# All large SBUF buffers moved by 128 bytes, and the two halves of a rounded weight pair set 4352 bytes apart

## The chip, the cores and the metric

One Trainium2 chip, one of its cores. The time is the device time of one execution in microseconds (us), from runs on the chip. Before the change: median 2161.43 us of 3 runs, 2159.44 to 2162.81.

## What is computed

Two layers of one kind of block, then one layer of another kind, on 512 tokens of width 1024, all in float32.

```python
for l in range(DEPTH):                       # DEPTH = 2
    proj = rms_norm(x, norm1[l]) @ w_in[l]   # 1024 -> 3148 columns, cut into the inputs of four attentions
    ...                                      # latent, sliding-window, top-k-selected and forget-gated attention
    x = x + mixed @ w_out[l]                 # 1024 x 1024
    x = x + jnp.square(jax.nn.relu(rms_norm(x, norm2[l]) @ w_up[l])) @ w_down[l]   # 1024 x 4096, 4096 x 1024
x = rms_norm(x, final_norm)
# second block, one layer
proj = (rms_norm_2(x, norm_w) * (1.0 + scale) + shift) @ w_in_2    # 1024 -> 9232 columns
y_a = gated_delta_rule(...) @ w_proj_a       # 8 heads, chunks of 64 tokens
y_b = dilated_window_attention(...) @ w_proj_b
x = x + gate * ((sigmoid(ga) * y_a + sigmoid(gb) * y_b) @ w_out)
```

The products with weight matrices are most of the work. The rest (norms, softmax, the delta rule's small matrices) is untouched by the change, apart from where its buffers lie.

## The kernel before

**A product in three.** A float32 operand is kept as two fp32r numbers, `high` (the value rounded) and `low` (what rounding left over). `product` (lines 179 to 183) makes a product out of three matmuls that add up in PSUM: L181 is high by high, L182 high by low, L183 low by high. The first argument after the output, `lhs`, is the stationary operand, which is loaded into the array ahead of the matmul; `rhs` is the moving one, which is streamed through, mostly 512 columns.

```python
    pe.matmul(out, lhs[0], rhs[0], start=start, stop=False)
    pe.matmul(out, lhs[0], rhs[1], start=False, stop=False)
    return pe.matmul(out, lhs[1], rhs[0], start=False, stop=stop)
```

Each of the three loads its stationary operand anew, L182 the same one as L181.

**Two forms.** `product_by_channels` (L877) and the inner loops at L1388, L2336, L2764 and L2941 have the weights stationary, 128 columns at a time, and stream the activations, 512 tokens: the trace prints these as `psum<-operand,weight_pairs` and `psum<-y_pair,weight_pairs`, the moving one first. `product_by_tokens` (L858) and the tail at L535 have 128 tokens of activations stationary and stream weight columns: `psum<-weight_pairs,hidden` (the MLP's down-projection, 512 columns), `psum<-weight_pairs,operand` (the out-projections, 512 columns, and narrower pieces of the in-projection). In both, a program's order is written out by hand, and each L18x follows the one before it with no other work of PE between, within a product.

**The ring of weights.** `WeightRing` (L94) holds `weight_ring`, 4 slots of raw fp32 (SLOT is 1056 elements, of which an item fills up to 1024), and `weight_pairs`, 3 slots of a high and a low half. SP sends an item into a raw slot (L140), ScalarE rounds it into the high half (L151), VectorE writes the low half (L160), and TensorE takes it (`take`, L163). The halves lie one SLOT apart: 4224 bytes.

**Where things lie.** Buffers are placed in SBUF one after another as they are declared, each at an offset that is the same in every partition. The first 16512 bytes hold a scratch area and constants. Then follow, in `program` (L3130), `x_stream` at byte 16512 (16384 bytes), `weight_ring` at 32896 (16896 bytes), `weight_pairs` at 49792 (25344 bytes) and `operand` at 75136 (32768 bytes). Each of these four starts is 128 more than a multiple of 256. The three slots of `weight_pairs` are 8448 bytes apart, which is 33 times 256, so every high half starts at 128 past a multiple of 256, and every low half, 4224 (16.5 times 256) further on, at a multiple of 256. `operand`, `hidden` and `y_pair` (both of whose starts are again 128 past one) keep their high and low parts 2048 bytes apart, so both of their parts start at 128 past a multiple of 256. Rows of 512 columns are 2048 bytes and tiles of 128 tokens 512 bytes long, so stepping through them keeps this remainder. In `latent_t` (L1409, 24 products of 96 stationary columns) it is 96, and in pieces of 96, 264 or 420 columns it changes from step to step.

Of the kernel before, what the change touches and what calls it, by code (L numbers as in the profile page):

```python
# [26 lines left out]
F32R = mybir.dt.float32r  # L27
# [5 lines left out]
P = 128  # L33
# [40 lines left out]
RING = 4  # L74
SPLIT_RING = 3
SLOT = 1056


class Chain:
# [3 lines left out]
    def __init__(self, eng, sem):  # L83
        self.eng, self.sem, self.n = eng, sem, 0
# [13 lines left out]
class WeightRing:  # L98
# [4 lines left out]

    def __init__(self, nc, ctx):
        self.buf = ctx.enter_context(nc.sbuf_tensor("weight_ring", [P, RING, SLOT], F32))
        self.pairs = ctx.enter_context(nc.sbuf_tensor("weight_pairs", [P, SPLIT_RING, 2, SLOT], F32R))
        self.landed = [ctx.enter_context(nc.semaphore(f"weights_landed_{i}")) for i in range(RING)]
        self.rounded = ctx.enter_context(nc.semaphore("weights_rounded"))
        self.split = ctx.enter_context(nc.semaphore("weights_split"))
        self.items_done = ctx.enter_context(nc.semaphore("items_done"))  # L110
        self.restart([])
# [780 lines left out]
def rows(w, k0, kk, c0, c1):  # L892

    return w[k0 * P:(k0 + kk) * P, c0:c1].rearrange("(k p) c -> p k c", p=P)


def for_tokens(w, chunks, c0, c1, k0=0):

    per = max(kk for kk in range(1, chunks + 1) if chunks % kk == 0 and kk * (c1 - c0) <= SLOT)
    return [rows(w, k0 + k, per, c0, c1) for k in range(0, chunks, per)]  # L900
# [37 lines left out]
def layer_items(l, w_in, mla_w_uq, mla_w_ukv, w_out, w_up, w_down):  # L938

    win, wuq, wukv, wout, wup, wdown = (w[l] for w in (w_in, mla_w_uq, mla_w_ukv, w_out, w_up, w_down))  # L940
    items = front_items(win, wuq, wukv)
    out_items = for_tokens(wout, KD, 0, 512) + for_tokens(wout, KD, 512, D)
    items += out_items
    for half in range(2):
        items += for_channels(wup, KD, half * KH * P, (half + 1) * KH * P)
        down_items = [i for c in (0, 512) for i in for_tokens(wdown, KH, c, c + 512, k0=half * KH)]
        items += down_items
    return items, len(out_items), len(down_items)
# [830 lines left out]
def second_masks(decay_mask, level_masks, window_incl_half, residues_half, window_incl, residues):  # L1779

    def build(pool, own):
        own(pool.memset(decay_mask[:], 0.0))
        own(pool.memset(level_masks[:], 0.0))
        for i, s in enumerate(LEVELS):
            own(pool.memset(level_masks[:, i, :].rearrange("p (j a w) -> p j a w", a=2, w=s)[:, :, 1, :], 1.0))
        own(pool.memset(window_incl[:], 0.0))  # L1790
        own(pool.memset(residues[:], 0.0))

        def keep(view, pattern, base, channel, fill):
            own(pool.affine_select(out=view, in_=view, compare_op=ALU.is_ge, fill=fill, base=base,
                                   pattern=pattern, channel_multiplier=channel))
        keep(decay_mask[:], [[1, P]], 0, -1, MASKED)
        for i, s in enumerate(LEVELS):
            half = level_masks[:, i, :].rearrange("p (j a w) -> p j a w", a=2, w=s)[:, :, 1, :]
            keep(half, [[-2 * s, P // (2 * s)], [0, s]], 0, 1, 0.0)
            keep(half, [[2 * s, P // (2 * s)], [0, s]], s - 1, -1, 0.0)  # L1800
        keep(window_incl[:], [[1, 2 * P]], 0, -1, MASKED)
        keep(window_incl[:], [[-1, 2 * P]], P, 1, MASKED)

        keep(residues[:], [[-1, P]], 0, 1, MASKED)
        keep(residues[:].rearrange("p (j w) -> p j w", w=32), [[32, 4], [0, 32]], 31, -1, MASKED)
        own(pool.tensor_copy(window_incl_half[:], window_incl[:]))
        own(pool.tensor_copy(residues_half[:], residues[:]))
    return build
# [812 lines left out]
def second_items(w_in, w_proj_a, w_proj_b, w_out):  # L2621

    one = lambda w: w.rearrange("o r c -> (o r) c")
    win, wa, wb, wout = (one(w) for w in (w_in, w_proj_a, w_proj_b, w_out))
    KB = wb.shape[0] // P

    def project(*names):
        return [i for n in names for i in for_channels(win, KD, COL_2[n], COL_2[n] + SPLITS_2[n])]

    items = [tuple(rows(win, 0, KD, COL_2[n], COL_2[n] + H) for n in ("a", "beta"))] + project("ka", "qa", "va")  # L2630
    n_conv = len(items)
    items += project("za", "ga", "zb") + project("vb", "qb", "kb") + for_channels(wa, KD, 0, D)
    items += project("gb") + for_channels(wb, KB, 0, D)
    out_items = for_tokens(wout, KD, 0, 512) + for_tokens(wout, KD, 512, D)
    return items + out_items, n_conv, len(out_items), KB
# [495 lines left out]
def program(nc, a, out):  # L3131
    with ExitStack() as ctx:
        def sb(name, shape, dtype=F32, ctx=ctx):
            return ctx.enter_context(nc.sbuf_tensor(name, shape, dtype))

        psum = ctx.enter_context(nc.psum_tensor("psum", [P, 8, 512], F32))
        x = sb("x_stream", [P, T, D])
        weights = WeightRing(nc, ctx)
        plans = [layer_items(l, *[a[n] for n in "w_in mla_w_uq mla_w_ukv w_out w_up w_down".split()])
                 for l in range(DEPTH)]  # L3140
        plan_2 = second_items(*[a[n] for n in "w_in_2 w_proj_a_2 w_proj_b_2 w_out_2".split()])
        weights.restart([i for plan in plans for i in plan[0]] + plan_2[0])
        operand = sb("operand", [P, KD, 2, S], F32R)
        small = sb("small", [P, 32])
        masks = (sb("decay_mask", [P, P]), sb("level_masks", [P, len(LEVELS), P]),
                 sb("window_incl_half", [P, 2 * P], BF16),
                 sb("residues_half", [P, P], BF16))
        modulated = sb("modulated", [P, KD])
        consts, vectors, vectors_2 = opening(nc, sb, psum, weights, x, operand, small, a)
        with ExitStack() as own:  # L3150
            def besides_last():
                modulation = Modulation(nc, ctx, a["ada_w_2"].rearrange("o r c -> (o r) c"), vectors_2[4],
                                        sb("modulation_sums", [P, 3, D], ctx=own),
                                        sb("ada_rows", [P, Modulation.SLOTS, D], ctx=own))
                return ((modulation, second_masks(*masks, sb("window_incl", [P, 2 * P], ctx=own), sb("residues", [P, P], ctx=own))),
                        (modulation, consts[1], vectors_2[0], modulated, vectors_2[3],
                         (a["ada_b_2"][:, D:2 * D], a["norm_w_2"], a["ada_b_2"][:, 2 * D:3 * D])))

            layers(nc, psum, x, operand, weights, consts, vectors, plans, small, besides_last, a)
        second_part(nc, psum, x, operand, weights, consts, vectors_2, masks, plan_2, small, out, a)  # L3160
# [24 lines left out]
```

## Time and profile before

| | |
|---|---|
| runs, median (lowest to highest) | 2161.43 us (2159.44 to 2162.81) |
| the profiled execution: span from first to last instruction | 2157.7 us |
| its own device time | not given apart; the lowest run stands 1.7 us above the span |
| TensorE busy | 2067.6 us, 96% of the span |
| VectorE, ScalarE, GpSimd busy | 1122.1, 836.3, 199.1 us |
| groups L181, L182, L183 together | 2360 of each, 7080 in all |
| HBM traffic | 180.74 MB read, 11.55 MB written |

How to read it: a matmul's printed duration runs from its start to a modelled end, and the next one starts before that end. What TensorE spends on one matmul in an unbroken run is the distance from its start to the next one's start. Starts in a timeline are rounded to 0.01 us.

### The profile page before, as it was taken

To read this page: it belongs to the slowest core of one execution; us is meant where nothing else is said; L and a number is where in the kernel's file an instruction comes from. 1 tells how busy PE (TensorE), PEld (TensorE's weight loads), DVE (VectorE), ACT (ScalarE), POOL (GpSimd) and SP (SyncE) were. 2 spreads that over 40 slices of the span, in tenths; PEclk is the share of its full clock that TensorE was granted. 3 is DMA by queue.
4 is the path that set the end of the run, shared out by engine and by line. 5 is a ranking of instruction groups with operands and counts; after the bars stand their busy time and mean duration, and the time that the engine had idled before them with its cause. 6 is when DMAs were issued, how large, how long until landed. Compare 5 with 4: busy or idle time off the path is not lost. (4 is left out here: it accounts for less than half of the span.)

```text
span 2157.7 us, 28306 instructions
## 1 busy us (share of the span) xinstructions
PE 2067.6 (96%) x10898; PEld 1685.8 (78%) x10902; DVE 1122.1 (52%) x1971; ACT 836.3 (39%) x1732; POOL 199.1 (9%) x169
## 2 busy tenths in 40 slices
PE   8999999999999999999999999799999999999997
PEld 7777777888887877777888887688787887777776
DVE  5787534423434498744552543578674333225545
ACT  4354633312323244643331332453433336324532
POOL 1331000000000143001000000002031330000100
PEclk9999999999999999999999999999999999999999
DMA  6321022232333432002542433223234223331232
GB/s 184 93 84 40 1 69 88 88 108 82 95 117 77 116 96 81 2 30 79 184 158 97 165 118 109 87 81 91 76 79 135 75 64 115 109 98 31 78 118 78
DMA packets 177527, 198.33 MB, mean 92 GB/s; under 512 B 38755, under 2 KB 140786, under 8 KB 176882
## 3 DMA queue, kind: packets, MB, share of 16 engines
q1 hardware_dynamic: 177394, 196.53, 29.6%
q8 instruction: 87, 1.43, 0.3%
q14 instruction: 46, 0.38, 0.1%
HBM read 180.74 MB, written 11.55 MB: 89 GB/s over the span
## 5 line engine op out<-in xcount | busy, mean ns | idle before, releaser
L160 DVE TENSOR_TENSOR weight_pairs<-weight_ring,weight_pairs 128x1024 fp32r<-128x1024 f32 (+4 forms) x293 | 355.7, 1217 | 446.7 <-ACT weight_pairs L151 446.0
L181 PE MATMUL psum<-operand,weight_pairs 128*128 128x512 f32 x1320 | 527.5, 400 | 18.8 <-PEq L203 13.9
L151 ACT ACTIVATE weight_pairs<-weight_ring 128x1024 fp32r<-128x1024 f32 (+4 forms) x293 | 303.4, 1038 | 577.7 <-PE psum L183 546.5
L183 PE MATMUL psum<-operand,weight_pairs 128*128 128x512 f32 x1320 | 527.1, 399 | 0.0
L182 PE MATMUL psum<-operand,weight_pairs 128*128 128x512 f32 x1320 | 525.9, 398 | 0.0
L181 PEld LDWEIGHTS psum<-operand,weight_pairs 128*128 128x128 f32 x1320 | 254.1, 192 | 84.4 <-issue 22.6
L182 PEld LDWEIGHTS psum<-operand,weight_pairs 128*128 128x128 f32 x1320 | 249.5, 189 | 55.1 <-issue 1.0
L183 PEld LDWEIGHTS psum<-operand,weight_pairs 128*128 128x128 f32 x1320 | 249.3, 189 | 54.0
L182 PE MATMUL psum<-weight_pairs,hidden 128*128 128x512 f32 x512 | 202.2, 395 | 0.0
L181 PE MATMUL psum<-weight_pairs,hidden 128*128 128x512 f32 x512 | 200.5, 392 | 0.0
L183 PE MATMUL psum<-weight_pairs,hidden 128*128 128x512 f32 x512 | 199.2, 389 | 0.0
L181 PE MATMUL psum<-weight_pairs,operand 128*128 128x512 f32 (+3 forms) x384 | 141.7, 369 | 7.2 <-DVE weight_pairs L160 3.7
L1097 DVE TENSOR_TENSOR mlp_work<-mlp_work 128x512 f32<-128x512 f32 x64 | 44.1, 689 | 187.9 <-ACT mlp_work L1080 187.9
L182 PE MATMUL psum<-weight_pairs,operand 128*128 128x512 f32 (+3 forms) x384 | 138.2, 360 | 0.0
L183 PE MATMUL psum<-weight_pairs,operand 128*128 128x512 f32 (+3 forms) x384 | 137.7, 359 | 0.0
L181 PEld LDWEIGHTS psum<-weight_pairs,hidden 128*128 128x128 f32 x512 | 95.9, 187 | 23.3 <-issue 0.2
L182 PEld LDWEIGHTS psum<-weight_pairs,hidden 128*128 128x128 f32 x512 | 96.2, 188 | 20.5 <-issue 0.2
L183 PEld LDWEIGHTS psum<-weight_pairs,hidden 128*128 128x128 f32 x512 | 96.1, 188 | 20.4
L1080 ACT ACTIVATE mlp_work<-psum 128x512 f32<-128x512 f32 x64 | 37.6, 594 | 141.3 <-PE psum L183 141.3
L726 DVE TENSOR_REDUCE stats<-psum 128x1 f32<-128x128 f32 (+3 forms) x176 | 66.6, 420 | 47.6 <-PE psum L665 44.6
L181 PEld LDWEIGHTS psum<-weight_pairs,operand 128*128 128x128 f32 x384 | 72.1, 188 | 21.6 <-issue 6.9
L822 ACT ACTIVATE probs<-psum,stats 128x128 f32<-128x128 f32 (+3 forms) x176 | 82.3, 477 | 9.9 <-DVE stats L732 5.5
(419 smaller groups left out, 2767.2 us busy)
## 6 DMA issues: line engine op xcount, KB each, us to landing
weight_ring<-in_w_in_dram SPq DMA_DIRECT2D x100, 512.0 KB, 3.6
weight_ring<-in_w_up_dram SPq DMA_DIRECT2D x64, 512.0 KB, 3.7
weight_ring<-in_w_down_dram SPq DMA_DIRECT2D x64, 512.0 KB, 3.5
weight_ring<-in_w_out_dram SPq DMA_DIRECT2D x24, 512.0 KB, 3.5
ada_rows<-in_ada_w_dram SPq DMA_DIRECT2D x24, 512.0 KB, 4.6
spilled<-v_t SPq DMA_DIRECT2D x22, 256.0 KB, 4.3
weight_ring<-in_w_in_dram SPq DMA_DIRECT2D x20, 256.0 KB, 2.9
weight_ring<-in_w_proj_a_dram SPq DMA_DIRECT2D x8, 512.0 KB, 3.4
```

Of the source, the lines that this page charges most:

```text
L151: act.activation(self.pairs[:, i % SPLIT_RING, 0, 0:n], self.buf[:, i % RING, 0:n], ACT.Copy).then_inc(self.rounded, 1)
L160: dve.tensor_tensor(self.pairs[:, i % SPLIT_RING, 1, 0:n], self.buf[:, i % RING, 0:n], self.pairs[:, i % SPLIT_RING, 0, 0:n].bitcast(F32), ...
L181: pe.matmul(out, lhs[0], rhs[0], start=start, stop=False)
L182: pe.matmul(out, lhs[0], rhs[1], start=False, stop=False)
L183: return pe.matmul(out, lhs[1], rhs[0], start=False, stop=stop)
L726: dve.tensor_reduce(stats[:, 4, j:j + 1], psum[:, j % SB, 0:jobs[j].width], AX_X, ALU.max).then_inc(found, 1)
L822: act.activation(probs[:, j % PB, 0:job.width], psum[:, j % SB, 0:job.width], ACT.Exp, bias=stats[:, 0, j:j + 1], scale=job.scale, accum_o ...
L1080: act.activation(self.relu[:, g % B, :], self.psum[:, g % 8, :], ACT.Relu).then_inc(self.rectified, 1)
L1097: dve.tensor_tensor(self.square[:, f % B, :], self.relu[:, f % B, :], self.relu[:, f % B, :], ALU.mult).then_inc(self.squared, 1)
```

## The change

`PAIR_SLOT`, 1088 elements or 4352 bytes (17 times 256), takes the place of SLOT in `weight_pairs`. A buffer `lines` of 128 bytes that nothing uses is declared ahead of `x_stream`. `x_stream`, `weight_ring`, `weight_pairs` then start at 16640, 33024 and 49920, which are multiples of 256; the high and the low halves of all three slots too, the slots being 8704 (34 times 256) bytes apart; `operand` starts at 76032, again a multiple of 256. Everything that is declared later lies 896 bytes further on, which is 128 more than a multiple of 256: what lay at 128 past a multiple of 256 lies on one now, and what lay on one lies at 128 past. No instruction is added, removed or moved, on any engine; the operands' addresses alone differ.

```diff
--- before.py
+++ after.py
@@ -74,6 +74,7 @@
 RING = 4
 SPLIT_RING = 3
 SLOT = 1056
+PAIR_SLOT = 1088
 
 
 class Chain:
@@ -103,7 +104,7 @@
 
     def __init__(self, nc, ctx):
         self.buf = ctx.enter_context(nc.sbuf_tensor("weight_ring", [P, RING, SLOT], F32))
-        self.pairs = ctx.enter_context(nc.sbuf_tensor("weight_pairs", [P, SPLIT_RING, 2, SLOT], F32R))
+        self.pairs = ctx.enter_context(nc.sbuf_tensor("weight_pairs", [P, SPLIT_RING, 2, PAIR_SLOT], F32R))
         self.landed = [ctx.enter_context(nc.semaphore(f"weights_landed_{i}")) for i in range(RING)]
         self.rounded = ctx.enter_context(nc.semaphore("weights_rounded"))
         self.split = ctx.enter_context(nc.semaphore("weights_split"))
@@ -3134,6 +3135,7 @@
             return ctx.enter_context(nc.sbuf_tensor(name, shape, dtype))
 
         psum = ctx.enter_context(nc.psum_tensor("psum", [P, 8, 512], F32))
+        sb("lines", [P, 32])
         x = sb("x_stream", [P, T, D])
         weights = WeightRing(nc, ctx)
         plans = [layer_items(l, *[a[n] for n in "w_in mla_w_uq mla_w_ukv w_out w_up w_down".split()])
```

## Rows read from the trace of the kernel before

**Rows 1.** The page of the profile: span, each engine's busy time, granted clock

```profile
span 2157.7 us, 28306 instructions
PE 2067.6 (96%) x10898; PEld 1685.8 (78%) x10902; DVE 1122.1 (52%) x1971; ACT 836.3 (39%) x1732; POOL 199.1 (9%) x169
...
PEclk9999999999999999999999999999999999999999
```

**Rows 2.** Waits of PE, the longest in total: us, times, longest us

```profile
PE psum L181 <- PEq L203: 20.8, 11, 5.1
PE psum L473 <- DVE mlp_work L460: 10.0, 4, 4.4
PE psum L181 <- DVE weight_pairs L160: 7.6, 4, 4.0
```

**Rows 3.** Groups by form, whole span: names, shapes, xcount | busy us, mean ns

```profile
L181 PE MATMUL psum<-operand,weight_pairs 128*128 128x512 f32 x1312 | 524.3, 400 | 17.6 <-PEq L203 12.7 <-DVE weight_pairs L160 4.0 <-ACT v_t L2403 0.7
L160 DVE TENSOR_TENSOR weight_pairs<-weight_ring,weight_pairs 128x1024 fp32r<-128x1024 f32 x260 | 319.2, 1231 | 424.2 <-ACT weight_pairs L151 423.6
...
L181 PE MATMUL psum<-weight_pairs,hidden 128*128 128x512 f32 x512 | 200.5, 392 | 0.0
...
L181 PE MATMUL psum<-weight_pairs,operand 128*128 128x512 f32 x192 | 76.5, 398 | 3.3 <-PEq L203 2.0 <-DVE weight_pairs L160 1.3
L182 PE MATMUL psum<-weight_pairs,operand 128*128 128x512 f32 x192 | 75.7, 394 | 0.0
...
L183 PE MATMUL psum<-weight_pairs,operand 128*128 128x512 f32 x192 | 75.3, 392 | 0.0
...
L181 PE MATMUL psum<-y_pair,weight_pairs 128*128 128x512 f32 x112 | 44.5, 397 | 4.9 <-PEq L203 4.9
```

**Rows 4.** Groups of PE from 340 to 420 us, the first MLP's up-projection

```profile
L183 PE MATMUL psum<-operand,weight_pairs 128*128 128x512 f32 x116 | 46.1, 397 | 0.0
L182 PE MATMUL psum<-operand,weight_pairs 128*128 128x512 f32 x116 | 46.0, 396 | 0.0
L181 PE MATMUL psum<-operand,weight_pairs 128*128 128x512 f32 x116 | 45.1, 389 | 0.0
```

**Rows 5.** Groups of PE from 430 to 510 us, its down-projection

```profile
L182 PE MATMUL psum<-weight_pairs,hidden 128*128 128x512 f32 x117 | 46.2, 395 | 0.0
L181 PE MATMUL psum<-weight_pairs,hidden 128*128 128x512 f32 x117 | 45.5, 389 | 0.0
L183 PE MATMUL psum<-weight_pairs,hidden 128*128 128x512 f32 x117 | 45.4, 388 | 0.0
```

**Rows 6.** Timeline of PE from 400 us: start us, us, engine, line, op, shapes

```profile
399.74 0.39 PE L181 MATMUL psum<-operand,weight_pairs 128*128 128x512 f32 x1
399.96 0.40 PE L182 MATMUL psum<-operand,weight_pairs 128*128 128x512 f32 x1
...
406.67 0.39 PE L181 MATMUL psum<-operand,weight_pairs 128*128 128x512 f32 x1
```

**Rows 7.** Timeline of PE from 450 us

```profile
449.64 0.40 PE L182 MATMUL psum<-weight_pairs,hidden 128*128 128x512 f32 x1
...
456.50 0.40 PE L182 MATMUL psum<-weight_pairs,hidden 128*128 128x512 f32 x1
```

**Rows 8.** Timeline of PE from 300 us, first out-projection

```profile
299.80 0.40 PE L182 MATMUL psum<-weight_pairs,operand 128*128 128x512 f32 x1
...
306.80 0.40 PE L182 MATMUL psum<-weight_pairs,operand 128*128 128x512 f32 x1
```

**Rows 9.** Timeline of PE from 2104 us, last out-projection

```profile
2103.68 0.40 PE L182 MATMUL psum<-weight_pairs,operand 128*128 128x512 f32 x1
...
2110.55 0.40 PE L182 MATMUL psum<-weight_pairs,operand 128*128 128x512 f32 x1
```

**Rows 10.** Timeline of PE near 160 us, products of unrounded fp32

```profile
160.17 1.88 PE L1487 MATMUL psum<-turned_qk,position_table 96*96 96x512 f32 x4
```

**Rows 11.** Groups of PE from 150.5 to 155.7 us, moving operand latent_t

```profile
L183 PE MATMUL psum<-latent_t,weight_pairs 128*96 128x512 f32 x7 | 2.8, 393 | 0.0
```

**Rows 12.** Timeline of PEld, the weight loads, from 400 us

```profile
399.97 0.19 PEld L183 LDWEIGHTS psum<-operand,weight_pairs 128*128 128x128 f32 x1
```

**Rows 13.** DMA issues: KB each, median us to landing

```profile
weight_ring<-in_w_up_dram SPq DMA_DIRECT2D x64, 512.0 KB, 3.7
```

## The prediction

> **What bounds the kernel now.** The page comes first: TensorE is busy for 2067.6 of 2157.7 us at a granted clock of nine tenths or more in every slice, while VectorE, the next engine, is busy for 1122.1 us [rows 1]. The idle 90 us are short waits at stage borders, the largest 20.8 us in all [rows 2]. So the kernel is as long as TensorE's stream of matmuls, and a change that moves no instruction can act in one way: by what a single instruction takes. The rows by form say where: L181 to L183 make 7080 matmuls, of which 1312 x 3 stream `operand` past stationary weights, 112 x 3 stream `y_pair`, 512 x 3 stream weights past `hidden`, and 192 x 3 stream weights past `operand` [rows 3].
>
> A printed duration (389 to 400 ns) overlaps the next matmul, so I take distances between starts. From 399.74 to 406.67 us lie 30 distances: 6.93 us, 231 ns each, 693 ns for the three of a product [rows 6]. In the down-projection 30 distances are 6.86 us, so 686 ns for three [rows 7]. In the first out-projection they are 7.00 us, 700 ns for three [rows 8]; in the last, with the same two buffers, 6.87 us, 687 ns [rows 9]. At the full clock of 2.4 GHz 512 columns are 213 ns; so 16 to 20 ns of each distance are not streaming.
>
> The printed durations show which of the three pays. In the up-projection L181 takes 389 ns, L182 396 and L183 397 [rows 4]; in the down-projection L181 389, L182 395, L183 388 [rows 5]. The modelled end adds about the same to each (389 - 227, from the split that follows), so their differences are those of the distances. Split by them, the down-projection's 686 ns are 3a + 6 - 1, so a, L181's distance, is 227 ns; the up-projection's 693 ns are 3a + 7 + 8, so a is 226.
>
> **Addresses beside these rows.** A matmul of a run has two readers of SBUF: its own moving operand, and the weight load of the next matmul, which starts 10 ns after it (399.96 us [rows 6] and 399.97 us [rows 12]). By the layout told above, all parts start at 128 past a multiple of 256, but for the low half of the weights, which starts on one. In the down-projection that half is what L182 streams, and L182 alone is slow. In the up-projection it is what is loaded during L182 and used by L183; L182 and L183 are slow. L181, which never has to do with it, has 389 ns in both. I read this as: **the two readers run 6 to 8 ns slower per matmul when their starts differ by half of 256 bytes**, with the load reaching over into the next matmul in the second form. `latent_t` starts at remainder 96, between the two, and is met by weights at both remainders: its L183 has 393 ns, between 389 and 397 [rows 11].
>
> **The change, part by part.**
> 1. *The 128 bytes ahead.* The three large operands move together, so moving and stationary high parts keep the same distance. By the reading above this is worth nothing by itself. Bounds: if the absolute remainder counts, each matmul can go to the slow or the fast value; that is priced as a rival.
> 2. *Halves 4352 bytes apart.* Now the low half too is at remainder 0, as everything else. All three of a product should have L181's distance, 226 to 227 ns, so 680 ns for three.
>    - Weights stationary, 1312 + 112 = 1424 products: 693 - 680 = 13 ns, 18.5 us.
>    - Down-projections, 512 products: 686 - 680 = 6 ns, 3.1 us.
>    - Out-projections, 192 products: the means 398, 394 and 392 stand 9, 5 and 3 ns above 389 [rows 3], together 17 ns: 3.3 us.
>    - Pieces of 264, 384 and 420 columns and `latent_t`: no row shows a clean pair. Their remainders shift too; by the nearest rows it is between -8 and +8 ns a product [rows 4], under 2 us for their some 230 products; I take nothing.
>    Sum 24.9 us. All of it is on the path, since these runs have no idle time in them ([rows 4], [rows 5] print 0.0).
> 3. *VectorE, ScalarE and DMA.* The low half's subtraction takes 1231 ns for an item, once in the 24 matmuls that an item feeds, some 5.5 us [rows 3]; a raw item of 512 KB lands 3.7 us after its issue and there are four slots [rows 13]. Their addresses move as well, by an amount that no row prices; a tenth either way, taken from nothing but caution, is covered by that slack and costs nothing. If the cover were gone, VectorE at 0.12 us more for 293 items would cost 35 us, but it is idle for half of the span.
> 4. *What is late next.* The waits at stage borders stay; where TensorE arrives earlier at one that another engine ends, the gain is lost. Of 90 us idle I let 1 us of the gain go there.
>
> So 24 us are taken from the median. The sum is made against the profiled span of 2157.7 us, to 2133.7; the runs lie 1.7 to 5.1 us above the span, and the forecast for the median is 2161.4 - 24 = **2137 us**, 1.1% less.
>
> What the pages say differs, and none of the sum rests on it. The Trainium skill's "SBUF — State Buffer", section "SBUF: two separate sides", says that TensorE has its own ports and never waits on anyone; by that the layout would do nothing and the time be 2161. It speaks of other engines, not of two readers within TensorE, and the rows with 389 and 397 ns for equal shapes do not agree with a reading that leaves no room for placement, unless the place in the group of three makes the difference.
>
> **The rivals.**
> - *The place in the group, not the address.* L181 is followed by a load of the same weights, L182 by other ones, L183 by new ones; the three are slow or fast for that. For: the pattern is as regular as this order is. Against: L183 takes 397 in one form and 388 in the other, both followed by new weights. Then nothing changes: 2161.
> - *The multiple of 256 is the slow start.* In all clean rows the part that is slow lies on a multiple of 256, and after the change all parts do. Then every matmul takes L182's or L183's distance, 234 ns (227 + 7), 702 for three: 1424 x 9 = 12.8 us, 512 x 16 = 8.2, and 192 products from about 697 (680 + 17) to 702, 1.0: 22 us more, 2183. Against: weights at both remainders beside `latent_t` give neither 389 nor 397, though half of them lie on the slow start [rows 11]. It decides from the first product on; there is no partial form.
> - *A run settles in a slower rhythm.* The same buffers gave 700 ns in one stage and 687 in another [rows 8, 9], so addresses alone do not fix the rhythm; something at the start of a run does. If equal starts favour the slower rhythm everywhere (700 for three), it is 1424 x 7 + 512 x 14 + 192 x 3 = 17.7 us more: 2179. Against: no stage with stationary weights shows it, and the down-projection does not either [rows 4, 5, 7].
> - *The whole 16 to 20 ns go.* Unrounded fp32 products of 512 columns at L1487: four records end 1.88 us after the first start, at 591 ns for the last, so three distances are 1.29 us, 430 ns each; if that is two passes, 215 ns a pass [rows 10]. With 215 ns for all, 1424 x 48 + 512 x 41 + 192 x 52 ns = 99 us less, 2062. Against: L181 has equal starts already and takes 227. The Trainium skill's "TensorE: Matmul & The Clock Gate", section "Back-to-back issue gap", gives N/2.4 + 2.5 ns, 216 ns for 512 columns, for a single matmul's gap; it names no address, and no fp32r row of this trace comes down to it.
>
> **How the numbers follow.** Equal starts are fast: 0.59. Nothing changes: 0.18. The multiple of 256 is slow: 0.11. Slower rhythm: 0.07. The whole gap goes: 0.05. Faster by over 0.2% (about what a measurement of this kernel can tell from no change): 0.59 + 0.05 = 0.64. Within: 0.17. Slower: 0.19, a hundredth of it for small losses of VectorE or the DMAs. The forecast's own range is 2124 (226 ns turns out to be 225, 7080 x 1 ns = 7 us, and narrow pieces gain 2, the medians' spread 3) to 2148 (half of the products with stationary weights keep their distance, 9 us). To hold 8 in 10 the range must take in no change, up to a few us beyond 2162: 2124 to 2169. The 0.05 below and nearly all of the 0.18 above from the two slow rivals stay out, a part of the slower rhythm (in some stages alone) lies inside.
>
> **What would show it.** In the changed profile the three means from 430 to 510 us and from 340 to 420 us should be equal within 2 ns, at 389, and 30 distances should be 6.80 us. TensorE's busy time should fall by about 24 us, its idle time stay near 90, VectorE's and ScalarE's means stay. Means of 396 and more on all three lines speak for the slow start or the slow rhythm; 389, 396 and 397 as before, for the place in the group. A mean under 386 would say that the gap itself depends on where parts start. A changed mean of L160 or a new wait for it would be a step that I have left out.

## The result, and the profile after

The changed kernel takes 2146.15 us against 2162.12 us before (medians of four runs each). One of its four runs took 2960.0 us at a granted clock of 0.647; the median of the other three is 2145.53 us, and by them the ratio is 0.992, with a 95% interval of 0.990 to 0.993. A repetition (below) gave 2142.73 us, ratio 0.991 [0.990, 0.992]. The change is worth 16 to 19 us; 24 were forecast.

The profiled execution took 2145.53 us. Its lines stand one further down: L182, L183 and L184 are the L181, L182 and L183 of before. The page of the kernel after:

```profile
span 2143.8 us, 28306 instructions
PE 2050.9 (96%) x10898; PEld 1685.0 (79%) x10902; DVE 1123.0 (52%) x1971; ACT 836.9 (39%) x1732; POOL 199.5 (9%) x169
...
PEclk9999999999999999999999999999999999999999
```

As many instructions were recorded as before, 28306. TensorE was busy for 16.7 us less than in [rows 1], VectorE and ScalarE as long as before. Groups of PE after, 340 to 420 us, then 430 to 510 us (count | busy us, mean ns | idle us):

```profile
L182 PE MATMUL psum<-operand,weight_pairs 128*128 128x512 f32 x119 | 46.3, 389 | 0.0
L183 PE MATMUL psum<-operand,weight_pairs 128*128 128x512 f32 x118 | 45.9, 389 | 0.0
L184 PE MATMUL psum<-operand,weight_pairs 128*128 128x512 f32 x118 | 45.9, 389 | 0.0
...
L183 PE MATMUL psum<-weight_pairs,hidden 128*128 128x512 f32 x119 | 46.3, 389 | 0.0
L184 PE MATMUL psum<-weight_pairs,hidden 128*128 128x512 f32 x118 | 45.9, 389 | 0.0
L182 PE MATMUL psum<-weight_pairs,hidden 128*128 128x512 f32 x118 | 45.9, 389 | 0.0
```

Six means of 389 ns stand where [rows 4, 5] had 389, 396, 397 and 389, 395, 388. The 80 us window holds 355 such matmuls instead of 348. Timeline of PE after, the first and the last start of 30 distances in the up-projection, then in the down-projection:

```profile
399.48 0.39 PE L182 MATMUL psum<-operand,weight_pairs 128*128 128x512 f32 x1
...
406.28 0.39 PE L182 MATMUL psum<-operand,weight_pairs 128*128 128x512 f32 x1
...
449.12 0.39 PE L182 MATMUL psum<-weight_pairs,hidden 128*128 128x512 f32 x1
...
455.92 0.39 PE L182 MATMUL psum<-weight_pairs,hidden 128*128 128x512 f32 x1
```

Both are 6.80 us, 226.7 ns each, as forecast; before they were 6.93 and 6.86 us [rows 6, 7]. Waits of PE after (us in total, times, longest):

```profile
PE psum L182 <- PEq L204: 20.6, 11, 5.2
PE psum L474 <- DVE mlp_work L461: 10.2, 4, 4.4
PE psum L182 <- DVE weight_pairs L161: 8.9, 4, 4.3
```

The waits are nearly those of [rows 2] (that for a split pair is 1.3 us longer in all); span less busy time is 92.9 us, and was 90.1. The subtraction of the low half and the landing of a raw item have not moved either (1218 ns over all its forms, 1217 before; 3.6 us where [rows 13] have 3.7), from the groups and the DMA issues of the page:

```profile
L161 DVE TENSOR_TENSOR weight_pairs<-weight_ring,weight_pairs 128x1024 fp32r<-128x1024 f32 (+4 forms) x293 | 356.0, 1218 | 442.3 <-ACT weight_pairs L152 441.9
...
weight_ring<-in_w_up_dram SPq DMA_DIRECT2D x64, 512.0 KB, 3.6
```

So both forms of product run in the forecast rhythm. Two questions are left: is it really the distance of two starts, and why were 16 to 19 us gained instead of 24?

### The profile page after: what moved, and what is told of

Its sections match the earlier page's. It is cut to its first block and busy times, and to the rows that moved or that the text cites. A ratio compares the mean times of both kernels' runs of the same rounds, so it can differ in the third digit from the quotient of the medians.

```text
span 2143.8 us, 28306 instructions
## 1 busy us (share of the span) xinstructions
PE 2050.9 (96%) x10898; PEld 1685.0 (79%) x10902; DVE 1123.0 (52%) x1971; ACT 836.9 (39%) x1732; POOL 199.5 (9%) x169
## 5 line engine op out<-in xcount | busy, mean ns | idle before, releaser
L161 DVE TENSOR_TENSOR weight_pairs<-weight_ring,weight_pairs 128x1024 fp32r<-128x1024 f32 (+4 forms) x293 | 356.0, 1218 | 442.3 <-ACT weight_pairs L152 441.9
L182 PE MATMUL psum<-operand,weight_pairs 128*128 128x512 f32 x1320 | 528.2, 400 | 19.1 <-PEq L204 13.7
L183 PE MATMUL psum<-operand,weight_pairs 128*128 128x512 f32 x1320 | 518.2, 393 | 0.0
L184 PE MATMUL psum<-operand,weight_pairs 128*128 128x512 f32 x1320 | 518.2, 393 | 0.0
L182 PEld LDWEIGHTS psum<-operand,weight_pairs 128*128 128x128 f32 x1320 | 250.0, 189 | 80.4 <-issue 23.7
L184 PEld LDWEIGHTS psum<-operand,weight_pairs 128*128 128x128 f32 x1320 | 249.4, 189 | 54.1
L183 PEld LDWEIGHTS psum<-operand,weight_pairs 128*128 128x128 f32 x1320 | 250.1, 189 | 51.1 <-issue 1.0
L182 PE MATMUL psum<-weight_pairs,hidden 128*128 128x512 f32 x512 | 200.1, 391 | 0.0
L184 PE MATMUL psum<-weight_pairs,hidden 128*128 128x512 f32 x512 | 199.3, 389 | 0.0
L183 PE MATMUL psum<-weight_pairs,hidden 128*128 128x512 f32 x512 | 199.2, 389 | 0.0
L182 PE MATMUL psum<-weight_pairs,operand 128*128 128x512 f32 (+3 forms) x384 | 141.3, 368 | 8.1 <-DVE weight_pairs L161 4.5
L184 PE MATMUL psum<-weight_pairs,operand 128*128 128x512 f32 (+3 forms) x384 | 137.7, 359 | 0.0
L183 PE MATMUL psum<-weight_pairs,operand 128*128 128x512 f32 (+3 forms) x384 | 137.6, 358 | 0.0
L182 PEld LDWEIGHTS psum<-weight_pairs,hidden 128*128 128x128 f32 x512 | 96.1, 188 | 20.2 <-issue 0.2
L184 PEld LDWEIGHTS psum<-weight_pairs,hidden 128*128 128x128 f32 x512 | 96.1, 188 | 20.1
L183 PEld LDWEIGHTS psum<-weight_pairs,hidden 128*128 128x128 f32 x512 | 96.1, 188 | 19.9 <-issue 0.2
L182 PEld LDWEIGHTS psum<-weight_pairs,operand 128*128 128x128 f32 x384 | 72.6, 189 | 21.3 <-issue 6.9
```

The costliest lines, as they stand in the source:

```text
L161: dve.tensor_tensor(self.pairs[:, i % SPLIT_RING, 1, 0:n], self.buf[:, i % RING, 0:n], self.pairs[:, i % SPLIT_RING, 0, 0:n].bitcast(F32), ...
```

## The experiments

**Theories.** A: the distance between the start of the moving operand and of the stationary one, modulo 256 bytes, sets the rhythm. B: the absolute start counts. C: the place in the group of three counts, or something that both parts of the edit do together.

### A map of distances

A program of its own, in place of the whole computation: 32 fp32r matmuls of 512 columns in a row for each pair of starts, two stationary tiles in turn, with one bf16 matmul between the groups.

```diff
+for mv in (0, 32):                  # moving operand at 0, at 128 bytes
+    for d in range(0, 64, 8):       # stationary one later by 0, 32, ... 224 bytes
+        run(mv, mv + d)
+for d in (1, 2, 4): run(0, d)       # by 4, 8, 16 bytes
+for d in (1, 2, 4, 8): run(d, 0)    # moving one later by 4, 8, 16, 32 bytes
+for m in (64, 16): for d in (0, 32): run(0, d, m=m)   # 64 and 16 stationary columns
+for d in (0, 16, 32, 48): run(0, d, cols=256)         # 256 moving columns
+for d in (0, 32): run(0, d, step=0)                   # one stationary tile throughout
+for d in (0, 32, 64): run_half(0, 2 * d)   # bf16, by 0, 128, 256 bytes
```

> A program of its own: it leaves out the whole computation and runs, on one engine, groups of 32 fp32r matmuls of 512 columns that each load 128 stationary columns, with the stationary operand 0, 32, 64 ... 224 bytes later than the moving one, first with the moving operand at a multiple of 256 bytes, then at 128 past one; then small differences of 4 to 32 bytes, fewer stationary columns, 256 moving columns, bf16, and one stationary tile throughout. Theory of the difference: the distance from start to start is about 227 ns at difference 0 and about 234 ns at 128, something between at the others, and the same in both sets; at some differences it might be under 227 ns. Theory of the slow start: 234 ns wherever an operand starts on a multiple of 256, 227 ns elsewhere. Theory of the place in the group: the same distance in every group, 227 to 234 ns. bf16 should show about 216 to 220 ns with no dependence, or the same dependence if the two readers hinder each other whatever the type.

Timeline of PE in the map, one row for a group of 32 (start us, us from the first start to the last end). The rows are, in order: stationary later by 0, by 32, by 128 and by 192 bytes; then both operands at 128 past, later by 0 and by 32; then bf16, later by 0 and by 128:

```profile
30.24 7.51 PE L70 MATMUL psum<-moving,still 128*128 128x512 f32 x32
...
37.63 7.72 PE L70 MATMUL psum<-moving,still 128*128 128x512 f32 x32
...
60.44 7.71 PE L70 MATMUL psum<-moving,still 128*128 128x512 f32 x32
...
75.62 7.59 PE L70 MATMUL psum<-moving,still 128*128 128x512 f32 x32
...
90.66 7.55 PE L70 MATMUL psum<-moving,still 128*128 128x512 f32 x32
...
98.09 7.72 PE L70 MATMUL psum<-moving,still 128*128 128x512 f32 x32
...
249.61 7.07 PE L76 MATMUL psum<-moving_half,still_half 128*128 128x512 bf16 x32
...
256.57 7.07 PE L76 MATMUL psum<-moving_half,still_half 128*128 128x512 bf16 x32
```

The first distance of a group is longer (0.31 to 0.34 us, behind the bf16 matmul), and its last matmul prints 0.39 to 0.40 us. So 30 distances are left: 7.51 us makes 227.0 ns a distance, 7.72 us 233.3, 7.59 us 229. Taken start by start, without the first three distances of each group, the means are:

```
stationary later by   0     32    64    96    128   160   192   224 bytes
moving at 0         226.7 233.3 233.4 234.3 233.3 233.2 229.1 233.4 ns
moving at 128       227.8 233.3 233.3 234.3 233.3 233.6 229.0 233.4
by 4, 8, 16 bytes: 232.4, 230.8, 233.4; moving later by 4, 8, 16, 32: 236.5, 233.4, 231.6, 233.4
```

The two lines agree within 0.4 ns, but for 1.1 at difference 0, where the group at 128 past began with some ten distances between 224 and 236 ns and then ran at 227. That is not the 128 bytes: in the finer map below the group at difference 0 with the moving operand at 0 begins in the same way and has the same mean, 227.8. Both follow a group with unequal starts. B falls: the slow-start rival is refuted, and moving both operands changes nothing. C falls too: here is no group of three, and the difference alone does it. But A was drawn wrongly in one point. Half of 256 bytes is not the bad distance; nearly every distance is bad, and 0 is the one good one, with a partial dip at 192. With fewer stationary columns the address matters less, and equal starts are less good: 64 columns take 229.8 ns at 0 and 231.1 at 128 bytes, 16 columns 228.8 and 231.9. The bf16 matmuls take 215.8 ns at differences of 0, 128 and 256 bytes. The Trainium skill's "TensorE: Matmul & The Clock Gate", section "Back-to-back issue gap", gives some 216 ns for 512 columns as the gap of an isolated matmul, and some 131 ns in a stream. The bf16 groups of this trace, which are streams, agree with the 216 (215.8) and not with the 131, and no fp32r group of 512 columns has a mean under 226.6.

### The halves alone, and the 128 bytes alone

The first leaves the 128 bytes out of the changed kernel, the second adds them alone to the kernel before:

```diff
-        sb("lines", [P, 32])
```

```diff
+        sb("lines", [P, 32])
```

> Only the distance of the halves is changed (4352 bytes); without the 128 bytes ahead, so all high and low parts start at 128 past a multiple of 256. Theory of the difference: as with the whole change, 389 ns on all three lines of a product, 2140 to 2148 us. If the multiple of 256 itself matters (aligned starts being better), it would stay nearer to 2155 us or the distances would come out 1 to 3 ns longer than with the whole change.

> Only the 128 bytes ahead are added, the halves stay 4224 bytes apart: high halves at multiples of 256, low halves 128 past one. Theory of the difference: nothing happens, 389, 396 and 397 ns in the up-projection as before, 2160 to 2164 us. Theory of the absolute start: the slow part changes from the low to the high half, so L182-like lines become fast and the other two slow, 680 + 7 ns a product in the second form, another time than before.

Halves alone: 2144.28 us, 0.992 [0.990, 0.994] of before, the whole gain. The 128 bytes alone: 2162.40 us over ten runs, 1.001 [1.000, 1.002]. Groups of PE from 340 to 420 us, with the halves alone, then with the 128 bytes alone:

```profile
L184 PE MATMUL psum<-operand,weight_pairs 128*128 128x512 f32 x118 | 45.9, 389 | 0.0
L182 PE MATMUL psum<-operand,weight_pairs 128*128 128x512 f32 x118 | 45.9, 389 | 0.0
L183 PE MATMUL psum<-operand,weight_pairs 128*128 128x512 f32 x118 | 45.9, 389 | 0.0
```

```profile
L183 PE MATMUL psum<-operand,weight_pairs 128*128 128x512 f32 x116 | 46.1, 397 | 0.0
L182 PE MATMUL psum<-operand,weight_pairs 128*128 128x512 f32 x116 | 45.9, 396 | 0.0
L181 PE MATMUL psum<-operand,weight_pairs 128*128 128x512 f32 x116 | 45.1, 389 | 0.0
```

With the 128 bytes alone every part has another absolute start than before, and every mean is as it was: step 1 of the prediction (worth nothing) holds.

### Every product opposed

The changed kernel with 128 more bytes between the weights and the activations, so that moving and stationary operands differ by 128 in all products, high and low.

```diff
+        sb("gap", [P, 32])          # ahead of operand
```

> The whole change, and 128 bytes more ahead of operand, so that every weight half lies at a multiple of 256 and operand, hidden and y_pair at 128 past one. Theory of the difference: all three lines take what the slow ones took before, 396 to 397 ns, so 700 to 702 ns a product in place of 681: 2128 products x 20 ns = 43 us more than with the whole change, 2185 to 2192 us. Theory of the place in the group, or any in which it only counts that all parts of a buffer have the same remainder: 2140 to 2150 us.

Measured: 2171.13 us over eight runs, 1.004 [1.003, 1.005] of before. Groups by form, whole span, of this kernel:

```profile
L183 PE MATMUL psum<-operand,weight_pairs 128*128 128x512 f32 x1312 | 521.9, 398 | 0.0
...
L182 PE MATMUL psum<-weight_pairs,hidden 128*128 128x512 f32 x512 | 203.4, 397 | 0.0
L184 PE MATMUL psum<-weight_pairs,hidden 128*128 128x512 f32 x512 | 202.4, 395 | 0.0
L183 PE MATMUL psum<-weight_pairs,hidden 128*128 128x512 f32 x512 | 202.4, 395 | 0.0
```

All lines are slow now, L182 included, which was fast in both kernels: the direction is A's, and slower than before, as it must be. The size was expected too large. Start by start, without waits, the distances are 232.5 to 233.4 ns: a product takes 697.8 ns with stationary weights, 699.0 in the down-projection and 697.9 in the out-projections. Before, they were 693.4, 688.0 and 695.3, so the rise is 1424 x 4.4 + 512 x 11.0 + 192 x 2.6 ns = 12.4 us; the medians differ by 9.4 us (from 2161.73). I had expected 43 us more than with the whole change, by 20 ns a product (700 to 702 instead of 681). It is 16 to 18 ns, because three slow distances in a row are some 233 ns each and not 234, and TensorE's busy time is 2085.4 us, 35 more than in the second profile of the changed kernel. The medians are only 26 to 28 us apart: the time that is not busy is 85.1 us here, against 90.9 and 92.9, and the clock 0.988 in the mean against 0.985.

### A finer map

```diff
+for d in (16, 48, 80, 112, ...): run(0, d / 4)
+for d in (0, 256, 512, 1024, 4096, 16384, 384, 640, 4224): run(0, d / 4)
+for d in (184, 200, 248, 252): run(0, d / 4)
+for n in (420, 384, 264): for d in (0, 64, 128, 192): run(0, d / 4, cols=n)
+run(0, 0, step=160); run(0, 32, step=160)   # every second stationary tile 128 bytes off
```

> Again a program of its own that leaves out the whole computation: groups of 32 fp32r matmuls, now with the stationary operand later than the moving one by 16, 48 ... 240 bytes, by 184, 200, 248 and 252, by 0, 256, 512, 1024, 4096 and 16384, by these plus 128, and with 420, 384 and 264 moving columns. Theory of the remainder by 256: 227 ns at every multiple of 256 up to 16384, 233 ns at each of them plus 128. Theory of whole distances: only 0, or only some of the multiples, gives 227. If the valley at 192 bytes (229 ns) is broad, 184 and 200 lie at 229 to 231 ns; if it is a point, at 233. Whether anything lies under 226 ns is open; if it does, it is worth 1 us for each 0.15 ns. The narrower pieces: with 256 columns 64 bytes gave 113 ns and 0 gave 120, so their best difference need not be 0.

Timeline of PE; the rows are: later by 0 and by 16384 bytes, by 384 bytes, then 420 columns, later by 0 and by 192:

```profile
129.06 7.54 PE L72 MATMUL psum<-moving,still 128*128 128x512 f32 x32
...
166.06 7.51 PE L72 MATMUL psum<-moving,still 128*128 128x512 f32 x32
...
173.45 7.68 PE L72 MATMUL psum<-moving,still 128*128 128x512 f32 x32
...
196.14 6.42 PE L72 MATMUL psum<-moving,still 128*128 128x420 f32 x32
...
215.06 6.30 PE L72 MATMUL psum<-moving,still 128*128 128x420 f32 x32
```

Differences of 256, 512, 1024, 4096 and 16384 bytes all give 226.6 or 226.7 ns, and 0 gives 227.8 with its slow beginning, 227 from there on; 384, 640 and 4224 all give 232.4, where 128 gave 233.3. So the remainder by 256 decides, within 1 ns and up to 16 KB apart, and no distance tried is better than 226.6. Between them: 16, 48, 112, 144, 208 and 248 bytes give 233.3 or 233.4 and 252 gives 233.6; 80 and 184 give 232.0, 200 gives 230.7, 176 gives 230.0, 240 gives 228.3. So the valley at 192 (229.1) is neither broad nor a point, as neither of the two expectations for it had it, and there is a second one at 240. The good place is a point, not the foot of a slope. Other widths have other good places: 420 columns take 193.3 ns at 0 and 188.8 at 192, 384 columns 173.4 at 0 and 173.2 at 192 against 176.6 at 64, 256 columns (in the first map) 119.8 at 0 and 113.4 at 64, and 264 columns 119.9 to 121.0 everywhere.

### The change again

The changed kernel, unaltered, beside new runs of the kernel before.

> The changed kernel as it is, for its time and granted clock over more runs. Theory that the faster stream spends more time at the lower clock: 2142 to 2147 us, mean clock 0.985 to 0.986, against 0.987 of the kernel before, and 21 to 22 us between the two at an equal clock. Theory that the low clock was chance: clock 0.987 and 2140 to 2142 us.

Measured: 2142.73 us, 0.991 [0.990, 0.992] of before, beside 15 runs of the kernel before. All four runs had a granted clock of 0.985. The 15 runs of before had 0.986 to 0.989, 0.987 in the mean. That is as the first theory had it, a faster stream with a lower clock.

This shows where to compare. The profiled execution of before (0.989) was one with an unusually high clock; the profile of the 128 bytes alone, which streams as before does, had 0.986. The page of the 128 bytes alone, then that of the change again:

```profile
span 2161.4 us, 28310 instructions
...
PE 2073.9 (96%) x10902; PEld 1690.7 (78%) x10902; DVE 1122.0 (52%) x1971; ACT 837.3 (39%) x1732; POOL 198.6 (9%) x169
```

```profile
span 2140.9 us, 28310 instructions
...
PE 2050.0 (96%) x10902; PEld 1681.9 (79%) x10902; DVE 1122.7 (52%) x1971; ACT 836.9 (39%) x1732; POOL 198.9 (9%) x169
```

Between these two TensorE's busy time falls by 23.9 us, not 16.7, and what is not busy grows from 87.5 to 90.9 us: 20.5 us in all. By the granted clocks of the traces, TensorE was at the lower of its two levels for 47 us in the profiled execution of before and for 61 us with the 128 bytes alone, against 68 and 65 us in the two of the changed kernel. So part of what the stream gained was lost to the clock in the first comparison.

### Waits filled, so that the clock stays up

TensorE works at the lower of its two levels, 1.2 GHz, for some microseconds after several of the long waits. Timeline of PE in the changed kernel, around one:

```profile
1870.49 0.39 PE L184 MATMUL psum<-operand,weight_pairs 128*128 128x512 f32 x1
1875.21 0.79 PE L182 MATMUL psum<-operand,weight_pairs 128*128 128x512 f32 x1 [4.33 <-DVE weight_pairs L161]
1875.80 0.63 PE L183 MATMUL psum<-operand,weight_pairs 128*128 128x512 f32 x1
1876.23 0.63 PE L184 MATMUL psum<-operand,weight_pairs 128*128 128x512 f32 x1
```

Its windows (us, PE busy, PEld, DVE, ACT, POOL, then the granted clock, DMA share, GB/s), a stretch after the wait:

```profile
1875.00:1879.00 4.00, 3.79 (x9) 3.02 (x10) 2.51 (x3) 1.75 (x2) 0.00 (x0) 0.50 0.53 172
```

Before the wait the starts are 0.23 us apart, after it 0.43 us, at a granted clock of 0.50. I supposed that such stretches had eaten the missing gain, and filled five long waits with small bf16 matmuls into a bank that is free, in both kernels alike. In front of three of the fills stands a wait until their bank is read out.

```diff
-            keep_busy(pe, self.psum[:, 4, :], self.ident_half, 24)
+            keep_busy(pe, self.psum[:, 4, :], self.ident_half, 24 if between is None else 96)
+            keep_busy(pe, psum[:, 0, :], HALF[-1], 90)       # ahead of the next projection
+            ...                                              # 44, 64 and 38 at three more stage ends
```

> The changed kernel, with bf16 matmuls of nothing (38 to 96 of 56 ns) put into five waits of TensorE of 2 to 5 us (before the last transpose of the last MLP's tail, at the end of the delta rule's stage, of the stage after it, of the gated products and of the merge weights). Theory that part of the gain is given back at the lower clock, which the waits bring on: clock 0.990 or more, 8 to 15 us less than the changed kernel, about 2133 us. Theory that the clock has nothing to do with these waits: the same clock, and 0 to 3 us more by matmuls that overshoot a wait.

> The kernel before with the same five fills, without the change. If layout and clock are two separate costs, it gains as much over the kernel before as the filled changed kernel gains over the changed one (8 to 15 us, about 2150 us), and the two filled kernels stand 21 to 25 us apart, the whole of what the address accounts for. If the fills only help the faster stream, it stays at 2160 us.

The changed kernel, filled: 2140.99 us, 0.990 [0.989, 0.992] of before, the fastest of all kernels here, at clocks of 0.989 to 0.993. The kernel before, filled: 2159.27 us, 0.9985 [0.998, 0.999], at 0.989 to 0.993. Of the 8 to 15 us that were expected from the fills, under 3 came in either kernel. Waits of PE in the filled kernel (lines another 3 further down):

```profile
PE psum L185 <- PEq L207: 15.2, 11, 2.2
PE psum L185 <- DVE weight_pairs L164: 9.4, 4, 5.6
```

The longest wait for PE's own queue fell from 5.2 to 2.2 us; the wait for a split pair near 1870 us grew from 4.33 to 5.63 us, and the lower clock after it stayed. It seems that what the fills let TensorE win earlier was partly waited for there, as it came early at weights that VectorE had not yet split; this was not tried by itself. In the whole span the lower level held for 34 us instead of 65, while 308 more matmuls ran. So the fills are a small gain on balance. They change the clock, the waits and the work at once, and what the lower clock alone costs can't be read from them.

At nearly equal clocks the change is worth about the same with and without them. At 0.984 to 0.986, the ten unfilled runs with equal starts (the change, its repetition, the halves alone) have a mean of 2143.9 us and the six with the 128 bytes alone 2163.7: 19.8 us. Their mean clocks are 0.9850 and 0.9857; among 32 runs of the kernel before, 0.001 more clock goes with 1.7 us less (12 runs at 0.986 have a mean of 2164.0 us, 4 at 0.989 of 2159.0), so at the same clock it would be some 21 us. At 0.993 the two filled kernels have 2138.1 (two runs) and 2156.5 (three): 18.4 us.

## Why the prediction was right, and where it was off

- **The time** was 2146 us where 2137 was forecast. The range of 2124 to 2169 took in no change as well, so the time alone says little for the mechanism; the distances and the runs with one part of the edit do.
- **The bound and the method** (distances between starts, split by the printed means) held: 6.80 us for 30, all six means 389. From 340 to 420 us of the kernel before, L181 to L183 are 226.7, 232.6 and 234.0 ns from start to start where they print 389, 396 and 397; from 430 to 510 us 226.7, 234.0 and 226.0 where they print 389, 395 and 388. So the split was right within 1 ns.
- **Step 1, the 128 bytes ahead: nothing.** Shown by the run with that alone, 1.001 [1.000, 1.002].
- **Step 2, the halves: 24.9 us.** Right in kind, 2 us too large. Start by start, a product went from 693.4 to 681.7 ns with stationary weights, 688.0 to 680.5 in the down-projection, 695.3 to 681.7 in the out-projections: 16.7 + 3.8 + 2.6 = 23.1 us. I took 680 ns for all after the change, and 697 before it in the out-projections. With stationary weights the mean is 227.2 ns, not 226.7: the first six distances of an unbroken run are 230.5 ns in the mean, those from the thirteenth on 226.7. The narrow pieces, taken at nothing, made under 1 us.
- **The reading behind it** was too narrow. "Run 6 to 8 ns slower when their starts differ by half of 256 bytes" is true (5 to 7 ns over the whole span), but so do they at nearly any difference other than 0. The conclusion survives, since it needed only that 0 is fast. `latent_t`, which I placed "between the two", differs from its weights by 32 and 160 bytes, both 233 ns in the map. Its L183 alone, which I showed, misled: start by start its three lines take 238.1, 230.9 and 230.9 ns, 233.3 in the mean, as slow as the map has it, and 233.0 after the change, when both differences are 32. The map has no group of 96 stationary columns, so how the three share it is not explained.
- **Step 3, other engines and DMA: nothing.** Their busy times and landings stayed.
- **Step 4, what is late next: 1 us.** Too small. Time that is not busy rose by 3.4 us between the two profiles at nearly equal clock. Over the unfilled profiles it is 85.1 (all products opposed), 87.5 and 90.1 us in the slower kernels, 89.3, 90.9 and 92.9 in the faster ones, so it rises where the stream is faster, but single profiles of the same stream differ by as much; this is a size, not a proof.
- **A term was missing: the granted clock.** I took it as given. It was 0.985 in the mean with the faster stream and 0.987 before. At 1.7 us for each 0.001 that is some 3 us between the medians; the runs at like clocks say 2 to 5 us (some 21 us, beside 16 to 19 between the medians). Why the faster stream gets less was not tried.
- So: 23 us of stream, less some 3 for waits, less some 3 for the clock, is 17, and the medians show 16 to 19. The last two terms are estimates, and no run separates them.
- **The rivals** fell as stated: the place in the group and the slow start by the map and by the 128 bytes alone; the slower rhythm exists, but at the beginning of a run only, and costs 2 to 3 us (681.7 ns instead of 680 in 1424 products); the whole gap does not go, no mean for 512 columns of fp32r is under 226.6.

## What to carry to other kernels

Where TensorE streams fp32r matmuls of 512 columns by 128 stationary ones back to back, put the moving operand and the stationary tile at the same remainder by 256 bytes, and check it for both halves of a rounded pair: where the halves lie an odd multiple of 128 bytes apart, one of them is always off. For other widths, measure first; the best remainder was another one for 256 and 420 columns. Look for it in the means of equal shapes, which should be equal; a pattern of 389, 396, 397 was worth 1% here. Moving everything together does nothing. Where a gain is under 2%, compare at equal granted clock (the clock varied here from 0.985 to 0.989 among runs of one kernel, with 1.7 us for each 0.001), and take a second profile before you look for a loss that the first one shows.

## What was not expected of the hardware

For 512 columns the good difference is a single point. Four bytes from it a distance is 232.4 ns, and 16384 bytes away 226.6. It is not the same point for all widths: for 420 columns 192 bytes is 4.5 ns better than 0, for 256 columns 64 bytes is 6.4 ns better. bf16 matmuls take 215.8 ns at every difference tried (0, 128 and 256 bytes). With one stationary tile used throughout, its repeated load is as sensitive (227.1 and 232.4 ns at differences of 0 and 128 bytes), and every second tile alone 128 bytes off makes all distances slow (233.4). What inside TensorE or at its reads makes this rhythm stays open: the runs show where it depends on addresses, not why.
